# A hybrid attention and mixture-of-experts block on one core: first norm two tiles ahead, and a reordered last row

## The reference, cut to what matters

```python
u = rms_norm(h, g_mix)
q, k, v, f_logit, b_gate, c_gate, hc = split(u @ w_in)
attn = rms_norm(forgetting_attention(norm(q), norm(k), v, log_sigmoid(f_logit + b_forget)), attn_out_g)
conv = rms_norm(b_gate * conv3(c_gate * hc), conv_out_g)
h = h + concat([attn, conv]) @ w_out
u2 = rms_norm(h, g_ffn)
# router: top-1 of 4 groups, then top-2 of its 8 experts, per token
# tokens sorted by expert into blocks of 128; each expert: (silu(x @ w_gate) * (x @ w_up)) @ w_down
h = h + sum over the 2 experts of gate * expert(u2)
```

## Time and the profile before

| | |
|---|---|
| median of three runs | 1296.54 us (1293.27 to 1296.95) |
| the profiled execution | 1293.03 us, its span 1291.0 us |
| PE busy | 1144.2 us, 89% of the span |
| DVE busy | 636.2 us, 49% |
| ACT busy | 540.1 us, 42% |
| POOL busy | 210.9 us, 16% |
| the chain that ended last | PE 59%, DMA 20%, DVE 8%, issue 6%, ACT 6% |
| moved by DMA | 291.54 MB, mean 226 GB/s |

### The profile page before, as it was taken

How to read it: one execution, slowest core, us unless ns; L and a number is a source line. 1 busy time by engine, 2 the same in 40 slices (tenths; PEclk the granted TensorE clock), 3 DMA queues, 4 the chain that set the end, 5 groups by cost and what they waited for, 6 DMA issues and landing times.

```text
span 1291.0 us, 18068 instructions
## 1 busy us (share of the span) xinstructions
PE 1144.2 (89%) x6636; PEld 861.8 (67%) x6636; DVE 636.2 (49%) x927; ACT 540.1 (42%) x811; POOL 210.9 (16%) x257
## 2 busy tenths in 40 slices
PE   4899999999898899999888999999998999999960
PEld 4899988899896566666666787655555555555530
DVE  6322234334435556656555986445444444455525
ACT  7212122044335445544432875444554444445520
POOL 4000001230200011011113022122221222222210
PEclk9999999999998899999998999999999999999995
DMA  9310004523004333222085899999999999999868
GB/s 257 99 67 1 1 33 135 191 101 123 10 1 122 87 86 83 79 81 72 17 359 183 326 377 380 418 421 397 400 390 389 406 408 401 398 397 397 357 252 332
DMA packets 66250, 291.54 MB, mean 226 GB/s; under 512 B 10696, under 2 KB 36328, under 8 KB 53648
## 3 DMA queue, kind: packets, MB, share of 16 engines
q1 hardware_dynamic: 48320, 243.91, 49.8%
q0 software_dynamic: 16720, 42.65, 8.9%
q10 hardware_dynamic: 1152, 4.19, 0.8%
HBM read 270.62 MB, written 37.92 MB: 239 GB/s over the span
## 4 chain that ended last, share of the span: by engine, by line
PE 59%; DMA 20%; DVE 8%; issue 6%; ACT 6%; SPq 1%; DVEq 0%; ACTq 0%; POOLq 0%
DMA wu<-in_w_up 17%; PE ps L1008 9%; PE ps L1010 9%; PE ps L1009 9%; PE ps L1349 4%; PE ps L1301 3%; PE ps L1303 3%; PE ps L1302 3%; PE ps L1089 2%; PE ps L1121 2%; PE ps L1103 2%; DMA y<-expert_rows 2%; PE ps L1290 2%; ACT wu_high L1634 1%; DVE probs L2033 1%
## 5 line engine op out<-in xcount | busy, mean ns | idle before, releaser
L2085 DVE TENSOR_TENSOR wu_low<-wu,wu_high 128x2048 fp32r<-128x2048 f32 x36 | 81.1, 2286 | 57.0 <-ACT wu_high L1634 57.0
L1315 PE MATMUL ps<-wu,xa 128*64 128x512 f32 x224 | 102.1, 598 | 0.0
L1315 PE MATMUL ps<-wg,xa 128*64 128x512 f32 x224 | 102.1, 598 | 0.0
L1634 ACT ACTIVATE wd_high<-wd 128x2048 fp32r<-128x2048 f32 x36 | 66.8, 1905 | 81.3 <-DMA wd<-in_w_down 79.4
L2085 DVE TENSOR_TENSOR wd_low<-wd,wd_high 128x2048 fp32r<-128x2048 f32 x36 | 81.2, 2287 | 36.0 <-ACT wd_high L1634 35.7
L1634 ACT ACTIVATE wu_high<-wu 128x2048 fp32r<-128x2048 f32 x36 | 66.9, 1907 | 69.9 <-DMA wu<-in_w_up 69.9
L1008 PE MATMUL ps<-uh,w_high 128*128 128x342 f32 (+1 forms) x256 | 87.5, 342 | 4.4 <-DVE w_low L1760 4.4
L2085 DVE TENSOR_TENSOR wg_low<-wg,wg_high 128x2048 fp32r<-128x2048 f32 x36 | 80.9, 2288 | 19.3 <-ACT wg_high L1634 19.3
L1010 PE MATMUL ps<-uh,w_low 128*128 128x342 f32 (+1 forms) x256 | 87.2, 341 | 0.0
L1009 PE MATMUL ps<-ul,w_high 128*128 128x342 f32 (+1 forms) x256 | 87.2, 340 | 0.0
L1634 ACT ACTIVATE wg_high<-wg 128x2048 fp32r<-128x2048 f32 x36 | 66.9, 1907 | 23.0 <-DMA wg<-in_w_gate 21.9
(11 more groups left out here) (380 smaller groups left out, 2919.5 us busy)
## 6 DMA issues: line engine op xcount, KB each, us to landing
wg<-in_w_gate SPq DMA_DIRECT2D x32, 2048.0 KB, 16.5
wu<-in_w_up SPq DMA_DIRECT2D x32, 2048.0 KB, 19.2
wd<-in_w_down SPq DMA_DIRECT2D x32, 2048.0 KB
u_rows<-u POOLq DMA_DIRECT2D x16, 512.0 KB, 6.1
y<-expert_rows SPq DMA_DIRECT2D x16, 512.0 KB, 12.2
raw_c<-in_w_in SPq DMA_DIRECT2D x5, 1024.0 KB, 5.3
xin<-in_x SPq DMA_DIRECT2D x8, 512.0 KB, 8.4
zx<-in_x POOLq DMA_DIRECT2D x4, 1024.0 KB, 6.6
```

The lines of the kernel that those rows point to most:

```text
L1315: last = mm(ps[HALF * n:HALF * (n + 1), 7, :], xa[:, k, :], raw[m][:, 1, k, :], start=(k == 0), stop=(k == KT - 1))
L1634: A(flat_half(wh[m][:, :, :], n), flat_half(raw_kf(m, s), n), ACT.Copy).then_inc(w_high[m], 1)
L2085: return V.tensor_tensor(flat_half(wl[m][:, s, :, :], n), flat_half(raw_kf(m, s), n), flat_half(wh[m][:, :, :], n).bitcast(F32), ALU.subtr ...
```

## The change

It has two parts.

**The start.** The issue of `gmix_b` moves from SP (third) to the front of ACT's block. ACT's norm keeps four slots in `ms`; `high_u` and `low_u` of a tile now stand behind the norm of the tile two later. The first weight chunk's two halves are set one before and one after the last tile's `high_u` and `low_u`. PE no longer waits for `params` before the channel products, and for `consts` only before the first `conv_mean`.

**The last row.** `GL` 1 moves on DVE from behind `GL` 0 to behind `U1` (the copy of the second half of the turned tokens). `U2` of R7 is made in two halves, and `U0` waits for the first alone. The unread products become 6 (from none) before `FIRST` of R6, 3 (from 12) before `U0`, 3 (from 4) before `L`.

```diff
-DVE_TAIL = [..., ("RT", R6), ("GL", 0), ("GL", 1), ("W0", R7),
-            ("G", R6), ("W1", R7), ("HOT", R6), ("U2", R7), ("FIRST", R6), ("S", R6), ("GT", R6), ("U0", R7), ("U1", R7),
+DVE_TAIL = [..., ("RT", R6), ("GL", 0), ("W0", R7),
+            ("G", R6), ("W1", R7), ("HOT", R6), ("U2", R7), ("FIRST", R6), ("S", R6), ("GT", R6), ("U0", R7), ("U1", R7), ("GL", 1),
             ("L", R7), ("LT", R7), ("RT", R7)]
-STREAMED = {..., ("W0", R7): 13, ("U0", R7): 12, ("L", R7): 4, ...}
+STREAMED = {..., ("W0", R7): 13, ("FIRST", R6): 6, ("U0", R7): 3, ("L", R7): 3, ...}
...
@@ SP
-            load_x(0)
-            load_x(1)
-            sp.dma_start(gmix_b[:, :], g_mix.partition_broadcast(P)).then_inc(gmix_in, 16)
-            for n in range(2, NT + 1):
+            for n in range(NT + 1):
                 load_x(n)
@@ PE
-                    pe.wait_ge(u2_ready, i + 1)
+                    if kind == "U0" and i == R7:
+                        pe.wait_ge(u2_first_half, 1)
+                    else:
+                        pe.wait_ge(u2_ready, i + 1)
...
-            pe.wait_ge(consts, 2)
-            pe.wait_ge(params, 16 * NPAR)
             for c in range(CT):
...
+                if c == 1:
+                    pe.wait_ge(consts, 2)
@@ ACT
+            act.dma_start(gmix_b[:, :], g_mix.partition_broadcast(P)).then_inc(gmix_in, 16)
...
-                if n >= 2:
-                    act.wait_ge(hn_ready, n - 1)
-                then(A(sqj[0:r, :], xin[0:r, n, :], ACT.Square, accum_out=ms[0:r, n % 2:n % 2 + 1]))
-                inv_root(ms[0:r, n % 2:n % 2 + 1], ms[0:r, n % 2:n % 2 + 1], 1.0 / D).then_inc(rs_ready, 1)
-                if n:
-                    high_u(toks[n - 1])
+                if n >= 4:
+                    act.wait_ge(hn_ready, n - 3)
+                then(A(sqj[0:r, :], xin[0:r, n, :], ACT.Square, accum_out=ms[0:r, n % 4:n % 4 + 1]))
+                inv_root(ms[0:r, n % 4:n % 4 + 1], ms[0:r, n % 4:n % 4 + 1], 1.0 / D).then_inc(rs_ready, 1)
+                if n >= 2:
+                    high_u(toks[n - 2])
+            high_u(toks[-2])
+            high_chunk(0, [0])
             high_u(toks[-1])
-            high_chunk(0)
+            high_chunk(0, [1])
             high_chunk(1)
@@ DVE
-                if n:
-                    low_u(toks[n - 1], n - 1)
+                if n >= 2:
+                    low_u(toks[n - 2], n - 2)
+            low_u(toks[-2], NT - 1)
+            low_chunk(0, [0])
             low_u(toks[-1], NT)
-            low_chunk(0)
+            low_chunk(0, [1])
...
+                        V.scalar_tensor_tensor(u2[:, 0:D // 2], h1b[:, 0:D // 2], ms[:, 2:3], gffn_b[:, 0:D // 2],
+                                               ALU.mult, ALU.mult).then_inc(u2_first_half, 1)
+                        V.scalar_tensor_tensor(u2[:, D // 2:], h1b[:, D // 2:], ms[:, 2:3], gffn_b[:, D // 2:],
+                                               ALU.mult, ALU.mult).then_inc(u2_ready, 1)
```

More of the change, by code:

```diff
@@ L125 @@
            ("LT", R7), ("G", R7), ("CNT", 0), ("FIRST", R7), ("KIND", 0)]
-DVE_TAIL = [("O", R7), ("LT", R6), ("N", R7), ("A", R7), ("AL", R7), ("RT", R6), ("GL", 0), ("GL", 1), ("W0", R7),
-            ("G", R6), ("W1", R7), ("HOT", R6), ("U2", R7), ("FIRST", R6), ("S", R6), ("GT", R6), ("U0", R7), ("U1", R7),
+DVE_TAIL = [("O", R7), ("LT", R6), ("N", R7), ("A", R7), ("AL", R7), ("RT", R6), ("GL", 0), ("W0", R7),
+            ("G", R6), ("W1", R7), ("HOT", R6), ("U2", R7), ("FIRST", R6), ("S", R6), ("GT", R6), ("U0", R7), ("U1", R7), ("GL", 1),
             ("L", R7), ("LT", R7), ("RT", R7)]
 ACT_TAIL = [("ASQ", R7), ("ARS", R7), ("AH", R7), ("GH", 0), ("GE", R6), ("URS", R7), ("U0", R7)]
-STREAMED = {("N", R7): 4, ("M", R7): 7, ("W0", R7): 13, ("U0", R7): 12, ("L", R7): 4, ("LT", R7): 2, ("G", R7): 10,
+STREAMED = {("N", R7): 4, ("M", R7): 7, ("W0", R7): 13, ("FIRST", R6): 6, ("U0", R7): 3, ("L", R7): 3, ("LT", R7): 2, ("G", R7): 10,
             ("FIRST", R7): 3, ("KIND", 0): 6}
@@ L525, in build @@
         u2_ready = sem("u2_ready")
+        u2_first_half = sem("first_half_of_last_u2")
         rows_out = sem("u2_rows_out")
@@ L1412, in inv_root, with high_chunk @@
                 return A(dst, dst, ACT.Exp, scale=-0.5)
+            act.dma_start(gmix_b[:, :], g_mix.partition_broadcast(P)).then_inc(gmix_in, 16)
             nc.scalar.preload_act_table_set("natural_log_exp_and_others")
-            def high_chunk(u):
+            def high_chunk(u, ns=range(2)):
                 act.wait_ge(win_in[u], 16 * (3 if u < CT else 1))
@@ L1428, in high_chunk @@
                     wait_made(act, last_job[u - 2])
-                for n in range(2):
+                for n in ns:
                     A(chunk_half(chunk_parts[u][0], u, n), chunk_half(chunk_raw[u], u, n),
@@ L1754, in bc, with low_chunk @@
                 return ap.unsqueeze(2).broadcast_to(shape)
-            def low_chunk(u):
-                for n in range(2):
+            def low_chunk(u, ns=range(2)):
+                for n in ns:
                     dve.wait_ge(chunk_high, 2 * u + n + 1)
@@ L1776, in _ @@
                     wait_made(dve, ("T", toks[n - 2]))
-                V.scalar_tensor_tensor(hn[0:r, n % 2, :], xin[0:r, n, :], ms[0:r, n % 2:n % 2 + 1],
+                V.scalar_tensor_tensor(hn[0:r, n % 2, :], xin[0:r, n, :], ms[0:r, n % 4:n % 4 + 1],
                                        gmix_b[0:r, :], ALU.mult, ALU.mult).then_inc(hn_ready, 1)
-                if n:
-                    low_u(toks[n - 1], n - 1)
+                if n >= 2:
+                    low_u(toks[n - 2], n - 2)
+            low_u(toks[-2], NT - 1)
+            low_chunk(0, [0])
             low_u(toks[-1], NT)
-            low_chunk(0)
+            low_chunk(0, [1])
             low_chunk(1)
@@ L1918, in extra @@
                         wait_x_made(dve, ("U1", i - 1))
-                    V.scalar_tensor_tensor(u2[:, :], h1b[:, :], ms[:, 2:3], gffn_b[:, :], ALU.mult,
-                                           ALU.mult).then_inc(u2_ready, 1)
+                    if i < R7:
+                        V.scalar_tensor_tensor(u2[:, :], h1b[:, :], ms[:, 2:3], gffn_b[:, :], ALU.mult,
+                                               ALU.mult).then_inc(u2_ready, 1)
+                    else:
+                        V.scalar_tensor_tensor(u2[:, 0:D // 2], h1b[:, 0:D // 2], ms[:, 2:3], gffn_b[:, 0:D // 2],
+                                               ALU.mult, ALU.mult).then_inc(u2_first_half, 1)
+                        V.scalar_tensor_tensor(u2[:, D // 2:], h1b[:, D // 2:], ms[:, 2:3], gffn_b[:, D // 2:],
+                                               ALU.mult, ALU.mult).then_inc(u2_ready, 1)
                 elif kind == "U0":
```

## The result

The changed kernel took 1286.19 us in the median of six runs (1282.89 to 1288.98), the kernel before 1295.70 in six (1292.73 to 1297.74). The ratio is 0.9918, with an interval of 0.9899 to 0.9938: **10.6 us faster** (8.0 to 13.1), where 6.5 were forecast. Repeated beside 23 runs of before (median 1296.81), it took 1284.64 in four runs, ratio 0.990 (0.9881 to 0.992). The profiled execution took 1283.55 us, its span is 1281.4; before it was 1291.0.

A forecast was written before the change was run, and what follows sets the result against it. The kernel was taken as one serial string of phases, with expert weight loads the chain's largest part after PE. Start 4.8 plus last row 1.7 made 6.5 us: 1296.54 to 1290.0, range 1285.5 to 1294.0.

The forecast's parts named there:

- the start's own term: Start, up to the channel products: PE's first product at 32.8 instead of 37.59, 4.8 us gained.
- 2.62 us a tile: Start: ACT's own norm (1.7) and copy (0.92) set the loop's pace, 2.62 us instead of 3.03.
- If one phase starts earlier, everything behind it follows: Whole kernel: a serial string of phases waiting on semaphores, so the start's 4.8 us carries through.
- rival D: Last row: PE's clock falls in short gaps, 2.5 us of work doubles; last row gains 1.2, sum 1290.5; chance 0.07.
- the store lands at about 684.0: Last row: the store of `u2` lands at 684.0, not 685.9, and releases the gather at 684.2.
- rival B: Last row: store lands at 685.9 as before, set by the weights' end; last row gains nothing, 1291.7; chance 0.22.
- The drain cannot come earlier: Last row: queues full of expert weights throughout, until 688; the second `wd`, issued 4.6 us sooner, just queues up.
- the gather lands at 690.1: Last row: gather slowed to a pace of 0.26 until 688, landing at 690.1 instead of 691.7; 1.7 us gained.
- work on the three engines from there on is the same: Last row: from `idxg`, 4.3 us sooner at 682.8, the three engines' work stays as before.
- A: Last row: gather not hindered by full queues, gaining 3.7 there; 8.5 in all, 1288.0; chance 0.14.
- C: Start: x tiles and `gmix_b` share the DMA engines, so the start gains only 2 to 3; 1292.3; chance 0.11.
- E: Last row: gather takes 15.4 us in full queues, landing 7.9 later; 3.1 us lost in all, 1299.6; chance 0.04.

The follow-up runs named there:

- mask_late: The changed kernel with POOL's first four mask adds held back until DVE is past its loop of `kn` multiplies; 1281.12 us in four runs, ratio 0.9886 to the kernel before.
- the three edits together: The changed kernel with second expert's last loads held, POOL's mask adds held, and unread products ahead of the channel products; 1279.40 us in six runs, ratio 0.988.
- warm_start: The changed kernel with eleven unread identity products on PE ahead of its wait for the channel weights; 1282.99 us in four runs, ratio 0.9899 to the kernel before.
- loads_held: The changed kernel with the second expert's two last weight loads (4 MB) held until the first gather has landed; 1283.14 us in four runs, ratio 0.9883.
- after_again: The changed kernel run once more, unchanged, for another profile; 1284.64 us in four runs, ratio 0.990 to the kernel before.
- start_only: The kernel before with only the start's edits of SP, PE, ACT and DVE, the last row as before; 1286.84 us, ratio 0.9921.

## Why the prediction was right or wrong

The sum was 4.8 + 1.7 = 6.5, and over four profiles of each kernel the spans differ by 11.1. Of the 4.6 that were missing, 0.5 are the start's own term, 1.3 a lead that grew behind it where the forecast put nothing, 1.1 the last row; the other 1.7 are tied to no edit (last paragraph).

**The start: right in mechanism, the term too small.** ACT does set the pace, and the third norm begins when its tile lands (8.49, predicted 8.2). Two steps were mis-sized. "2.62 us a tile" is 2.51: from a square to the next root there are 1.61 us, not the 1.7 that I read across the signal to DVE. So the ninth root is at 24.6, not 25.0. Then "with some 0.05 us between instructions" was 0.5 in all, where the rows have 0.09 between the end of the last `ul` and PE. First product 32.03 for 32.8. My starting point was also one profile at 37.59 where four have a mean of 37.43. In all 5.4 against 4.8.

**"If one phase starts earlier, everything behind it follows": the step that failed.** The 5.3 became 6.6 by 344 us, since POOL's adds are released by a transfer and DVE's loop is not, so a shift of one against the other changes how often they meet. With no collision at all (`mask_late`, and the three edits together) the lead grows by 3.1; the changed kernel has 1.3 of these by luck. `warm_start` shows that it's the phase and no merit of the change, since another shift gives the 1.3 back. Why the transfer ahead of the adds took 10.6 us instead of 9.0, and so decided the phase, I did not find; with `gmix_b` on SP it took 10.6 too, and with the unread products 9.0 again.

**The last row: right for 1.7 by two errors that cancelled, then 1.1 more.** `U2` was 1.8 us sooner (predicted 1.85), the second copy 4.5 (4.5), `idxg` 3.9 (4.3). (In three of the four profiles of before it stands at 34.2, against which the gain is 3.3 to 3.7.) In two profiles of after, 0.4 of it was lost to PE's clock (rival D, below).

Then "the store lands at about 684.0", 1.9 sooner like its issue, was wrong. It was issued 1.7 sooner and landed 0.8 sooner (33.8 to 33.0, the mean of landings between 31.9 and 35.5 before, and between 32.5 and 33.1 after): the latency grew from 13.5 to 14.4. This is rival B's half: the store lands when the weights have drained, as `loads_held` shows. "The drain cannot come earlier" was wrong as well, by about 1 us: counted from the end of attention, the DMA share is still 0.90 from 33.3 to 35.3 before, and 0.33 from 33.8 to 35.8 after. In one profile of before the store had already been the last wait (`idxg` at 34.2, gather at 35.8). So the gather started 2.5 us sooner, not 3.7. And "the gather lands at 690.1", at a pace of 0.26 until 688, was wrong the other way: by then the queues were nearly empty (that 0.33, in 681 to 683), so the gather took 4.66 us to PE's first use on average against 4.46 before. (The 3.85 us that I took for the gather before were short, too: in the other three profiles of before it landed after 4.4 to 4.5.) A wall that holds the store back is gone when the gather goes. The Trainium skill's rule of turns by packet ("DMA: Bandwidth & Descriptors", section "Queues, rings and completion order") would have given 2.3, which is what the gathered rows gained, but no run here shows that it acts: the gather had little to share with.

Last, "work on the three engines from there on is the same" failed for PE: from the gathered rows to the first `silu` it took 13.4 us before and 13.0 after on average, and from 10.5 to 14.0 over all profiles. The products of the first block run at the lower clock until it rises, before until about 702, after until about 693.

**Rival D** came in part, at a smaller price. In two of the four profiles of after the granted clock was at its lower level from 19 us after the end of attention, for 3.4 us, as in three of before, and the router's products took longer:

```profile
670.09 2.65 PE L1161 MATMUL ps<-u2T,wr 128*40 128x128 f32 x16
...
678.89 0.58 PE L1183 MATMUL ps<-first_code,rank_hot 128*128 128x2 f32 x4 [0.33 <-DVE cnt L2122]
```

(`after_again`, to be set against 1.91 and 0.99 in the rows of the changed kernel.) In the two others, the shown one among them, it held there, and fell only behind the idle at 673 to 675 that the router's choice leaves; then the products ahead of `idxg` took 0.99 us instead of 0.58. The 0.7 us that the first kind loses cost nothing. In the second kind DVE came to `rk` 0.8 us sooner, but `rk` then took 1.11 us instead of 0.28 and ended with POOL's memset of `xg`, which stands at the same place in all four, so that both kinds go on at 25.7 us from the end of attention. The 0.4 of the second kind stayed: all six profiles of this kind, with the last row's change, have `idxg` at 30.9, and all four of the first at 30.5. D's price was 2.5 us; `idxg` still came 3.3 to 3.7 sooner. **A** had one half: the gather was hardly hindered once it was issued, but it started 2.5 us sooner and not 3.7. **C and E** did not come: the start was not fed by DMA, and the gather took 4.6 to 4.8 us, not 15.4.

**The median against the trace.** I took the 3.5 us that the profiled run lay under the median as given. The first profile was in fact a lucky one in attention (242.8 against 245.7), so differences to it alone read too small. Over four profiles each the spans differ by 11.1 us, and the medians by 9.5 and 12.2 (the first ratio makes it 10.6). Of the 11.1, the 1.1 in attention, the -0.4 in the blocks and the 1.1 behind the last one are not tied to any edit, and stay open.

## What to carry to other kernels

Where an alternation of two engines has a wait in it, put the copy two steps behind and count the new pace from one engine's own instructions, start to start; that forecast held within 5%. The store queued behind 12 MB of loads had no latency of its own: it landed when the loads had drained. So hold part of the load (here the hold brought the first `silu` 2.4 us forward), or try to issue the transfer before it, which no run here tested; and then look whether the lead is still there where the next loads set the pace, as here it was not. And before believing that a lead is carried on unchanged, look at where two engines that are released by different things touch the same ports, since a shift moves their collisions.

## What the runs showed of the hardware that was not expected

- A DVE multiply of 128x256 with both operands in SBUF went from 0.42 to as much as 2.47 us beside POOL's adds of 2.4 us; one small `tensor_scalar` (`rk`) from 0.28 to 1.11 us, ending at 672.98, just behind POOL's memset (671.10 + 1.83 = 672.93).
- Nineteen fp32r products of 342 columns stood 0.285 us apart at the lower clock and 0.157 at the full one. Unread products in the wait ahead of them (28.80 to 31.4) kept a clock that was already up, and the first product ran at full clock; left idle, PE lost it at 31.9 in `start_only` and made the first eleven at the lower level. That is 2 us at the first copy, for nothing.
- The granted clock of a stretch says nothing where the trace has no record of it: in the kernel before it reads 1.00 in 38 to 40, while eight products are done there, 0.285 apart, the pace of the lower level; the first record of that trace stands at 40.5. The distance of equal products tells the level there.
